# Hybrid decoder step: 16 more tokens of the expert layer through gathered rows

## The reference

```python
def peer_ffn(xn, lp):
    q = (x @ lp['peer_wq']).reshape(N, PEER_HEADS, 2, PEER_DHALF)
    s = jnp.einsum('nhcd,ckd->nhck', q, lp['peer_subkeys'])
    v1, i1 = lax.top_k(s[:, :, 0], PEER_TOPK)
    v2, i2 = lax.top_k(s[:, :, 1], PEER_TOPK)
    cand = (v1[..., :, None] + v2[..., None, :]).reshape(N, PEER_HEADS, PEER_TOPK * PEER_TOPK)
    sc, ci = lax.top_k(cand, PEER_TOPK)
    idx = e1 * N_KEYS + e2                  # e1, e2: keys of the chosen candidates
    gate = jax.nn.softmax(sc, axis=-1)
    ...
        hid = jnp.einsum('td,thkd->thk', xb, u_tab[ib])
        hid = jax.nn.gelu(hid, approximate=False) * gb
        return jnp.einsum('thk,thkd->td', hid, v_tab[ib])
```

## Time and profile before

| | us |
|---|---|
| median of three runs | 2512.45 |
| runs | 2505.97 to 2513.10 |
| profiled execution, time | 2507.41 |
| profiled execution, span | 2506.0 |
| pick, from the first weights to the last copy | 931 to 1243 |
| spread | 1243 to 1447 |
| experts | 1447 to 2491 |
| store | 2491 to 2506 |

### The profile page before, as it was taken

How to read it: one execution, slowest core, us unless ns; L and a number is a source line. 1 busy time by engine, 2 the same in 40 slices (tenths; PEclk the granted TensorE clock), 3 DMA queues, 4 the chain that set the end, 5 groups by cost and what they waited for, 6 DMA issues and landing times. The chain is left out here.

```text
span 2506.0 us, 44410 instructions
## 1 busy us (share of the span) xinstructions
PE 2276.2 (91%) x16793; PEld 2019.3 (81%) x16793; DVE 1637.8 (65%) x3508; ACT 789.2 (31%) x1372; POOL 813.3 (32%) x651
## 2 busy tenths in 40 slices
PE   2999898897698879999899969999999999999998
PEld 2999897775434877776588669999999999999998
DVE  2672474546782535998499447777777677777775
ACT  1422232214322211112277533333333333333331
POOL 2000000000130000333100046666666666676672
PEclk8999899888898889999899979999999999999999
DMA  2223001212484221213239877787786777787781
GB/s 67 74 77 123 32 4 41 71 52 86 130 296 146 75 63 55 79 64 117 91 101 233 235 280 268 274 307 254 274 305 254 279 260 266 285 318 270 294 300 49
DMA packets 252154, 428.89 MB, mean 171 GB/s; under 512 B 81029, under 2 KB 181824, under 8 KB 237281
## 3 DMA queue, kind: packets, MB, share of 16 engines
q1 hardware_dynamic: 206433, 264.20, 32.5%
q0 software_dynamic: 45568, 162.63, 17.3%
HBM read 383.10 MB, written 43.68 MB: 170 GB/s over the span
## 5 line engine op out<-in xcount | busy, mean ns | idle before, releaser
L2644 POOL TENSOR_TENSOR experts_VL<-experts_V,experts_VH 128x2048 fp32r<-128x2048 f32 x64 | 295.8, 4622 | 296.7 <-ACT experts_VH L2573 296.5
L2530 PE MATMUL experts_pV<-experts_GH,experts_VH 128*128 128x392 f32 x1024 | 363.3, 355 | 0.3 <-DVE keep_xT L2689 0.3
L2530 PE MATMUL experts_pV<-experts_GH,experts_VL 128*128 128x392 f32 x1024 | 348.6, 340 | 0.0
L2530 PE MATMUL experts_pV<-experts_GL,experts_VH 128*128 128x392 f32 x1024 | 348.2, 340 | 0.0
L2689 DVE TENSOR_TENSOR keep_xT<-experts_pV,keep_xT 128x392 f32<-128x392 f32 x512 | 282.1, 560 | 77.0 <-PE experts_pV L2530 77.0
L2519 PE MATMUL experts_pH<-keep_xh,experts_UH 128*128 128x392 f32 x704 | 242.7, 345 | 0.0
L2519 PE MATMUL experts_pH<-keep_xl,experts_UH 128*128 128x392 f32 x704 | 241.1, 343 | 0.0
L2519 PE MATMUL experts_pH<-keep_xh,experts_UL 128*128 128x392 f32 x704 | 240.6, 342 | 0.0
L2567 ACT ACTIVATE experts_UH<-experts_pU 128x512 fp32r<-128x512 f32 x176 | 105.0, 597 | 346.0 <-PE experts_pU L2507 346.0
L2530 PEld LDWEIGHTS experts_pV<-experts_GH,experts_VH 128*128 128x128 f32 x1024 | 192.8, 188 | 1.0 <-DVE keep_xT L2689 0.6
L2530 PEld LDWEIGHTS experts_pV<-experts_GL,experts_VH 128*128 128x128 f32 x1024 | 193.1, 189 | 0.0
(11 more groups left out here) (429 smaller groups left out, 5179.7 us busy)
## 6 DMA issues: line engine op xcount, KB each, us to landing
experts_V<-in_peer_v SPq DMA_DIRECT2D x64, 1024.0 KB, 6.2
experts_U<-in_peer_u SPq DMA_DIRECT2D x44, 1024.0 KB, 8.4
scratch_gates<-spread_M SPq DMA_DIRECT2D x3, 7680.0 KB, 35.8
experts_M<-scratch_gates SPq DMA_DIRECT2D x64, 360.0 KB, 3.1
keep_K<-in_cache_k SPq DMA_DIRECT2D x64, 256.0 KB, 3.4
keep_V<-in_cache_v POOLq DMA_DIRECT2D x64, 256.0 KB, 4.0
front_w<-in_w_in SPq DMA_DIRECT2D x30, 512.0 KB, 3.8
pick_U<-in_peer_u SPq DMA_DIRECT2D x24, 512.0 KB, 3.7
```

Of the source, the lines that this page charges most:

```text
L2530: last = nc.tensor.matmul(bank(q, n)[:, 0:DT], l, r, start=(t == 0), stop=(t == 5))
L2644: nc.gpsimd.tensor_tensor(VL[q.b][:, :, :], V[q.b][:, :, :], VH[q.b][:, :, :].bitcast(F32), ALU.subtract).then_inc(v_lo, 1)
```

## The change

16 more tokens (the last 16, eight of them decoded ones) leave the dense part, which has 376 columns instead of 392. They are *wide*: their 16 tokens x 8 heads lie on the 128 partitions, so one gathered row for each of 16 choices serves them all, and K grows from 128 to 144 rows of U and of V.

- pick scores four groups instead of five for a head. The wide tokens' queries are copied aside (q16, one copy ahead of each of the 16 query copies), scored once behind the last head (score_wide) and taken through a ninth round of choice. At its end nine copies, one for each group and quantity, stand for three.
- spread has 94 units instead of 98; the third piece has 104 columns instead of 120.
- experts makes a copy of each wide token for each head (yw), turns it into rows (xw) with eight more turns, uses xw and yw as operands of the last 16 rows of either half, and has rows as in the new share: none in a body whose next pair is early, eight shares where the pair after next is early, six otherwise; up to three stand ahead of each gating.
- store has six pieces, of 112, 112, 112, 40, 128 and 16 tokens; the last one sums yw over the heads by a matmul with head.

```diff
-DT = TQ - SPARSE
-NJ = TT - 1
-WD = DT // NJ
+WIDE = 16
+DT = TQ - SPARSE - WIDE
+UNITS = [(0, 125), (125, 125), (250, 126), (DT, SPARSE)]
...
-SPREAD = [(0, 120), (120, 120), (240, 120), (360, 32)]
+SPREAD = [(0, 120), (120, 120), (240, 104), (344, 32)]
...
                 for e in range(2):
-                    for j in range(TT):
-                        last = nc.tensor.matmul(pS[0:w, 2 * j + e, :], qT[:, e, j * WD:j * WD + P], kT[:, e, :],
-                                                start=True, stop=True)
+                    for j, (t0, n) in enumerate(UNITS):
+                        last = nc.tensor.matmul(pS[0:w, 2 * j + e, :], qT[:, e, t0:t0 + P], kT[:, e, :], start=True, stop=True)
+                last.then_inc(scored, 1)
+
+            def score_wide():
+                for e in range(2):
+                    last = nc.tensor.matmul(pS[0:w, 2 * UN + e, :], q16[:, e, :, :].rearrange("p h t -> p (h t)"), kT[:, e, :],
+                                            start=True, stop=True)
                 last.then_inc(scored, 1)
...
+                sc(nc)(q16[:, e, h, :], acc[:, 1, h2 - WIDE:h2], ACT.Copy)
                 sc(nc)(halves3(qT[:, e:e + 1, :]), acc[:, :, 0:h2], ACT.Copy).then_inc(queried, 1)
...
+                if h == PH - 1:
+                    act.wait_ge(scored, PH + 1)
+                    sc(nc)(Sw[:, :, :], pS[0:w, 2 * UN:2 * UN + 2, :], ACT.Copy).then_inc(copied, 1)
...
             for q in range(3):
-                sc(nc)(eT[:, q, :].rearrange("p (j t) -> p j t", j=NJ), pS[:, q * NJ:(q + 1) * NJ, 0:WD], ACT.Copy).then_inc(taken, 1)
+                for j, (t0, n) in enumerate(UNITS[:-1]):
+                    sc(nc)(eT[:, q, t0:t0 + n], pS[:, 3 * q + j, 0:n], ACT.Copy).then_inc(taken, 1)
...
-            for h in range(PH):
-                g = h % 2
-                if h + 1 < PH:
+            for h in range(PH + 1):
+                g, u = h % 2, units(h)
+                if h < PH:
                     best_of_halves(h + 1)
...
-    K = PH * TOPK
+    KS = PH * TOPK
+    K = KS + TOPK
...
-            return 0 if n == TURN else 1 if Pair(n + 1).early else 5
+            return 0 if n == TURN or Pair(n + 1).early else 8 if Pair(n + 2).early else 6
...
+            if not q.after(1) and n < 2:
+                pe.wait_ge(x_rows, n + 1)
             pe.wait_ge(added, q.count(ND, n + 1))
...
                 last.then_inc(x_turned, 1)
+                pe.wait_ge(x_each, 1)
+                for b in range(2):
+                    for k in range(4):
+                        each = yw[:, (4 * b + k) * P:(4 * b + k + 1) * P]
+                        last = nc.tensor.transpose(pV[b][:, k * P:(k + 1) * P], each, c["ident"][:, :])
+                    last.then_inc(x_turned, 1)
                 for st in range(4):
                     turn(pe, Pair(0), st)
...
+                for b in range(2):
+                    act.wait_ge(x_turned, b + 2)
+                    sc(nc)(xw[:, b * 512:(b + 1) * 512], pV[b][:, :], ACT.Copy).then_inc(x_rows, 1)
...
-            pool.wait_ge(x_turned, 1)
+            pool.wait_ge(x_turned, 3)
...
+            x, y = (pX, pX) if n % K < KS else (xw, yw)
             if n < K:
-                nc.vector.scalar_tensor_tensor(out=row[n % SLOTS], in0=row[n % SLOTS], scalar=1.0, in1=pX[:, :],
+                nc.vector.scalar_tensor_tensor(out=row[n % SLOTS], in0=row[n % SLOTS], scalar=1.0, in1=x[:, :],
...
-                nc.vector.scalar_tensor_tensor(out=pX[:, :], in0=row[n % SLOTS], scalar=hid[:, n - K:n - K + 1], in1=pX[:, :],
+                nc.vector.scalar_tensor_tensor(out=y[:, :], in0=row[n % SLOTS], scalar=hid[:, n - K:n - K + 1], in1=y[:, :],
...
             dve.sem_inc(added, 3)
+            nc.vector.tensor_copy(yw[:, :].rearrange("p (k h t) -> p k h t", k=KD, h=PH),
+                                  xn[:, :, DT + SPARSE:TQ].unsqueeze(2).to_broadcast([P, KD, PH, WIDE])).then_inc(x_each, 1)
...
-            dve.wait_ge(x_turned, 1)
+            dve.wait_ge(x_rows, 2)
+            nc.vector.memset(yw[:, :], 0.0)
...
-                    for one in range(0 if q.early else 2):
+                    for one in range(0 if q.early else 3):
                         if mine:
                             use_row(dve, mine.pop(0))
                     gate(dve, q, e)
...
-STORED = [(j * WD, WD) for j in range(NJ)] + [(DT, SPARSE)]
+STORED = [(0, 112), (112, 112), (224, 112), (336, DT - 336)] + [(DT, SPARSE), (DT + SPARSE, WIDE)]
...
+                if j == LAST:
+                    pe.wait_ge(heads, 1)
+                    nc.tensor.matmul(pt[n % 4][0:w, :, :], head[:, :], yw[:, 512 * half:512 * half + 512].rearrange("p (q d) -> p q d", q=4),
+                                     start=True, stop=False)
```

More of the change, by code:

```diff
@@ L1934, in peer_choose @@
     h2 = TQ // 2
+    UN = len(UNITS)
+    units = lambda h: UN if h < PH else 1
     wv = ins["peer_wq"][0].rearrange("(c p) n -> p c n", p=P)
@@ L2066, in _ @@
             for q in range(3):
-                for j in range(NJ):
-                    last = nc.tensor.transpose(pS[:, q * NJ + j, 0:WD], ex[0:WD, j, q, :, :].rearrange("p h k -> p (h k)"),
-                                               c["ident"][0:WD, 0:WD])
+                for j, (t0, n) in enumerate(UNITS[:-1]):
+                    last = nc.tensor.transpose(pS[:, 3 * q + j, 0:n], ex[0:n, j, q, :, :].rearrange("p h k -> p (h k)"),
+                                               c["ident"][0:n, 0:n])
             last.then_inc(turned, 1)
@@ L2142, in _ @@
             look(PH // 2 - 1, 0)
+            pairs(PH // 2, 0, 1)
             look(PH // 2 - 1, 1)
+            look(PH // 2, 0, 1)
         @blk.vector
@@ L2167, in best_of_halves @@
                 dve.wait_ge(copied, h + 2)
-                for j in range(TT):
-                    top16([(v[g][:, j, e, :], ix[:, j, e, :], S[g][:, 2 * j + e, :], S2[e][:, :]) for e in range(2)])
+                scores = S[g] if h < PH else Sw
+                for j in range(units(h)):
+                    top16([(v[g][:, j, e, :], ix[:, j, e, :], scores[:, 2 * j + e, :], S2[e][:, :]) for e in range(2)])
             def indices(h):
-                nc.vector.tensor_copy(ixf[h % 2][:, :, :, :], ix[:, :, :, :]).then_inc(halved, 1)
+                nc.vector.tensor_copy(ixf[h % 2][:, 0:units(h), :, :], ix[:, 0:units(h), :, :]).then_inc(halved, 1)
                 dve.wait_ge(halved, h + 3)
@@ L2177, in key_indices @@
                     dve.wait_ge(looked, 2 * h + e + 1)
[L2178 removed]
+                    found = ex[:, :, e, h, :] if h < PH else exw[:, :, e, :]
+                    chain(nc.vector.tensor_reduce(found, one[e][:, 0:units(h), :, :], AX.X, ALU.add))
             best_of_halves(0)
             indices(0)
[L2182 to L2184 removed]
+            for h in range(PH + 1):
+                g, u = h % 2, units(h)
+                if h < PH:
                     best_of_halves(h + 1)
@@ L2407, in peer_experts @@
         spent, own = s.sem("spent"), s.sem("own")
-        x_hi, x_lo, x_turned = (s.sem(n) for n in ("x_hi", "x_lo", "x_turned"))
+        x_hi, x_lo, x_each, x_turned, x_rows = (s.sem(n) for n in ("x_hi", "x_lo", "x_each", "x_turned", "x_rows"))
         blk = s.block()
@@ L2756, in _ @@
         def _(pe):
-            for n in range(2 * TT):
+            for n in range(2 * N):
                 j, half = n // 2, n % 2
@@ L2761, in _ @@
                     pe.wait_ge(copied, n - 3)
+                if j == LAST:
+                    pe.wait_ge(heads, 1)
+                    nc.tensor.matmul(pt[n % 4][0:w, :, :], head[:, :], yw[:, 512 * half:512 * half + 512].rearrange("p (q d) -> p q d", q=4),
+                                     start=True, stop=False)
                 for q in range(4):
-                    last = nc.tensor.transpose(pt[n % 4][0:w, q, :], acc[:, 4 * half + q, t0:t0 + w], c["ident"][:, :])
+                    x = acc[:, 4 * half + q, t0:t0 + w]
+                    if j < LAST:
+                        last = nc.tensor.transpose(pt[n % 4][0:w, q, :], x, c["ident"][:, :])
+                    else:
+                        last = nc.tensor.matmul(pt[n % 4][0:w, q, :], x, c["ident"][:, :], start=False, stop=(q == 3))
                 last.then_inc(turned, 1)
@@ L2767, in _ @@
         def _(dve):
-            for n in range(2 * TT):
+            nc.vector.tensor_reduce(head[:, :], c["ident"][:, :].rearrange("p (h t) -> p t h", h=PH), AX.X, ALU.add).then_inc(heads, 1)
+            for n in range(2 * N):
                 j, half = n // 2, n % 2
@@ L2786, in _ @@
                 sp.dma_start(outs["y_prompt"][0, t0:t0 + prompt, :], rows[j % 2][0:prompt, :]).then_inc(stored[j % 2], 16)
-            sp.dma_start(outs["y_sample"][:, 0, :], rows[NJ % 2][SPARSE - DEC:SPARSE, :]).then_inc(stored[NJ % 2], 16)
-            sp.wait_ge(stored[0], 64)
-            sp.wait_ge(stored[1], 32)
+            sp.dma_start(outs["y_sample"][:, 0, :], rows[LAST % 2][WIDE - DEC:WIDE, :]).then_inc(stored[LAST % 2], 16)
```

(2 more changed lines are left out.)

117 lines of the change are left out of this document (69 added, 48 removed).

## The result

The changed kernel takes 2486.97 us (median; 2482.26 to 2494.57), the kernel before 2511.9 us beside it: ratio 0.9907, 95% interval 0.9886 to 0.9927. It is faster, by 25 us, where 41 were forecast. At the scale of the 2512.45 us of the first table, 0.9907 is 2489 us, just above the range.

The account below looks back on a forecast made before the run. TensorE was taken to set the end of three stages, the DMA engines that of spread. Terms -36 - 15 + 9 + 8 - 7 - 1.5 + 1.5 = -41 from 2507.4 us gave 2466.4, said as 2467 us; range 2446 to 2488.

Parts of the forecast that it names:

- Columns: Experts: 5184 U and V matmuls go from 392 to 376 columns, saving TensorE time; -36 us.
- The rival of weight loads: Experts: weight loads pace the matmuls, so fewer columns give nothing; 2498 us, 2513 without the saved waits; chance 0.05.
- Old waits: Experts loop: TensorE's 18 waits for VectorE's low parts of U go with the new places of rows; -15 us.
- New waits: Experts: 32 more rows make VectorE late, mostly in V-half bodies that multiply U without a turn; +9 us, ends 0 and 15.
- The wide rows' operands: Experts: VectorE rows with SBUF operands and GpSimd's subtraction of V hold each other up in two bodies; +8 us.
- exclusion in full: Experts rival: VectorE waits out a 4.62 us subtraction in each of five wide-row bodies; +23 for +8, 2482 us; chance 0.20.
- Pick and spread: Pick: fewer score passes and columns, less new copies, -7 us. Spread: 94 units for 98, -1.5 us, ends -6 and 0.
- Store: Store stage: six stores for five, one more round through the two buffers; +1.5 us, ends 0.5 and 3.
- Start of the stage: Experts start: eight more turns and copies delay the first turn of U, covered by the first U load; nothing counted.
- Late rows: Experts rival: fuller DMA engines land gathered rows late, so VectorE waits; 66 us lost, 2533 us; chance 0.05.

Follow-up runs that it names:

- PSUM variant: The changed kernel with the operands of the wide rows of both halves in PSUM (pX) instead of SBUF; 2462.3 us, ratio 0.9823.
- the kernel before alone: The kernel before with only the new order of rows, still 128 rows and 392 dense columns; 2494.85 us, ratio 0.9955.
- the PSUM variant with the rows apart: The PSUM variant with rows among the additions of C bodies (U product, no turn) moved from behind additions 0, 1, 2 to 2, 5, 7; 2461.61 us, ratio 0.9790.
- the plain instructions: The PSUM variant with four plain VectorE instructions added ahead of the second gating in four U-half bodies; 2489.65 us, ratio 0.9906.
- the old order at 144 rows: The PSUM variant with the order of rows turned back to the old one; 2493.62 us, ratio 0.9916.
- the kernel before with SBUF operands: The kernel before with the last 16 of its 128 rows in either half on SBUF operands; 2523.12 us, ratio 1.0058.
- the run with the U half alone in PSUM: The changed kernel with only the 16 wide U rows' operands in PSUM, the V half unchanged; 2472.15 us, ratio 0.9858.

## Why the prediction was right or wrong

**Columns: right.** -36 forecast. The spacing fell from 0.1789 to 0.1721 us; 6.8 ns x 5184 = 35.2. The loops give the same: the PSUM variant is 40.1 us shorter than before, of which 15.8 is the order of rows, and its periods in the V half and at its ends are 10.4 us over the 44.86 of the U half: 40.1 - 15.8 + 10.4 = 34.7. The rival of weight loads as the bound fell with the spacing.

**Old waits: right**, -15 forecast, -15.8 measured in the kernel before alone. What the sum could not show is that they would have grown to 26 us or more.

**New waits: right, though the trace shows less idle time than was forecast.** +9 forecast. The periods of the V half in the PSUM variant are 10.4 us over those of the U half, 1.2 of it VectorE's copy of pX (1.21 us in its trace), so 9.2. The wait that answers to the earlier trace rows, here in the changed kernel, is shorter than the 1.06 us worked out:

```profile
2172.85 0.44 PE L2568 MATMUL experts_pV<-experts_GH,experts_VH 128*128 128x376 f32 x1 [0.36 <-DVE keep_xT L2736]
```

0.52 with the 0.16. But the matmuls of the product before it start late as well, by some 0.27 us that no wait is shown for, and the following ones a little: the period with three rows is 1.04 us over, that with two 0.43. The forecast had 1.06 and 0.5.

**The wide rows' operands: the step that failed.** The term was +8: "I take two of the other four, about 4 us each". Measured: 22.4 us between the two kernels, 23.6 with the 1.2 us that the PSUM variant pays for that copy. Two things were mis-sized. First, all four bodies were hit, not two. Where two things become ready at the same moment, one order was counted as free. In three bodies the subtraction came first, by 0.04 to 0.12 us, and VectorE was held. In the fourth VectorE came first: GpSimd was held, and VectorE's next wide row met the subtraction right behind. Only the body with two wide rows had no such next row, and it escaped. Second, the price was taken as idle time alone (15.6 us, 16.2 with the 0.16). The clock behind each stall was left out: it was 0.79, 0.62, 0.62 and 0.79 over the 8 us behind the four, 9.4 us at most, and brought the price to 23.6. The upper end of 23 us was reached, by other addends than the 5 x 4.62 that it was worked out from; that they agree is luck. The rival "exclusion in full", 2482 us at a chance of 0.20, is what happened: its gain of 25 us is the gain that was measured.

The sentence on the Trainium skill (SBUF — State Buffer, Who interferes with whom) stood beside that rival: it says that whoever issues first holds the shared ports for the whole instruction and the other is fully blocked. The runs agree: 5.61 us for a row that lasts 1.22 beside nothing, 5.47 for a subtraction that lasts 4.62, and no effect at all on rows with one operand in PSUM. The row of 6.35 us, which got no turn between several instructions of GpSimd, goes beyond it.

The evidence of before was weighed too lightly: the eight multiplications of 4.07 to 4.11 us each start 0.15 to 0.17 us behind the start of a comparison by VectorE with two SBUF operands. And it was not read to the end. The prediction says that the trace shows no VectorE instruction that waited; it shows one, a subtraction at pick's end, whose operands are both pick_best, beside the last two of these multiplications (the last line is a product of the same size with nothing beside it):

```profile
1204.03 3.52 DVE L2204 TENSOR_TENSOR pick_ex<-pick_best 128x640 f32<-128x640 f32 x1
...
1202.80 7.52 POOL L2132 TENSOR_TENSOR pick_one<-pick_one,pick_ixf 128x1280 f32<-128x1280 f32 x2 [14.27 <-DVE pick_one L2201]
...
1238.54 0.82 DVE L2210 TENSOR_TENSOR pick_ex<-pick_ex,pick_z 128x640 f32<-128x640 f32 x1
```

It lasts 3.52 us and ends at 1207.55, 0.68 us behind the first of the two multiplications (1206.87).

**Pick and spread: nearly right.** -8.2 for -7 and -3.4 for -1.5. **Store: mis-sized**, +3.1 for +1.5, just over its upper end of 3: the sixth round has a product with 16 columns ahead of each copy (1.26 us of wait in the last one) on top of the store's landing.

**Start of the stage: the cover didn't hold.** The eight turns and two copies ahead of the first turn of U were costed at nothing, "what would show there is 1 to 2 us". It is 1.6.

**Late rows: fell.** Gathers landed in 4.2 to 18.3 us, median 9.0, with the DMA engines at 0.83 instead of 0.75, and VectorE waited for none of them.

The sum with what the runs showed, loop alone: -34.7 - 15.8 + 9.2 + 23.6 = -17.7, as measured. It closes by construction, since the 34.7 is what the loops leave over; its test is the 35.2 of the spacing.

**A version better than both** is the PSUM variant with the rows apart: 0.979 of the kernel before, where the change itself gave 0.991. Whether it is faster than the PSUM variant alone (0.982) is open: the intervals overlap, though its loop is 2.3 to 2.9 us shorter in the profiled executions.

## What to carry to other kernels

Before an operand of a VectorE instruction moves from PSUM to SBUF, look what GpSimd runs beside it; if both read SBUF, take the full price, in every body, however unlikely the meeting looks: all four bodies with three such rows in a line were hit here, whichever engine came first. Price a stall of a busy TensorE at more than its idle time: read the granted clock behind it. And where several edits act on one queue, test them one at a time and together: the order of rows was worth 16 us by itself and 26 beside the others.

## What the runs showed of the hardware that was not expected

A stall of TensorE of 2.7 to 4.6 us was followed, in the three windows shown here and in that behind the second stall of the plain instructions (0.79), by a granted clock of 0.57 to 0.79 over some 8 us; the six such stalls of the U halves cost 4.6 to 7.4 us each. Shorter ones could do the same: the longest wait with the old order at 144 rows, 1.93 us, and two of 2.2 us in the U half of the kernel before with SBUF operands were each followed by 0.79. The old waits of 0.5 to 1.3 us, 18 of them, left the clock of their windows at 1.00. Nor did the length of a stall alone set the clock behind it: waits of 3.77 and 4.50 us were followed by 0.62 and 0.79 in the changed kernel, and waits of the same lengths by 0.79 and 0.63 in the run with the U half alone in PSUM.

When GpSimd's subtraction was cut in four, a row of VectorE with two SBUF operands mostly got its turn behind one quarter, but one row waited for all that GpSimd had in line, 6.35 us.

A store of 125 rows of 4 KB made the next copy wait 5.56 us, one of 112 rows 2.53. Why was not tried: the size of the piece and the way its rows are divided changed together.
